# An encoder layer whose first projection takes its operands from a transposed copy of x

## What is computed

```python
u = rms_norm(h, g_pre_mix[l])     # h * rsqrt(mean(h*h) + EPS) * g
proj = jnp.einsum('bsd,de->bse', u, w_in[l])
sq, sk, sv, rx, rg, cq, ck, cv = jnp.split(proj, split_idx, axis=-1)
```

## Time and profile before

| | |
|---|---|
| median of 3 runs | 1148.42 us (1148.1 to 1149.21) |
| the profiled execution | 1147.69 us, its span 1146.0 us |
| TensorE busy | 1080.7 us (94%) |
| VectorE, ScalarE, GpSimd busy | 805.1, 574.7, 78.5 us |
| granted TensorE clock, mean | 0.974 of full speed |
| DMA | 70.44 MB, mean 61 GB/s |
| first projection matmul (L677) | 16.99 us after the span's start |

### The profile page before, as it was taken

How to read it: one execution, slowest core, us unless ns; L and a number is a source line. 1 busy time by engine, 2 the same in 40 slices (tenths; PEclk the granted TensorE clock), 3 DMA queues, 4 the chain that set the end, 5 groups by cost and what they waited for, 6 DMA issues and landing times.

```text
span 1146.0 us, 12155 instructions
## 1 busy us (share of the span) xinstructions
PE 1080.7 (94%) x4844; PEld 843.8 (74%) x4844; DVE 805.1 (70%) x778; ACT 574.7 (50%) x711; POOL 78.5 (7%) x70
## 2 busy tenths in 40 slices
PE   6999999997899999979999999999999999999993
PEld 5777777886445447857888888878888878888782
DVE  2535668656454544879778686799876898867998
ACT  6313432447455551575675446743466533467353
POOL 0004113201100101410000000000000000000000
PEclk9999999978899999988999999999999999999997
DMA  7221112110000025140220401301204013026003
GB/s 223 59 65 38 37 37 74 37 38 1 1 1 1 1 85 191 74 166 1 78 69 1 147 1 37 110 1 60 88 1 147 1 37 111 1 62 232 1 1 147
DMA packets 44640, 70.44 MB, mean 61 GB/s; under 512 B 10244, under 2 KB 19752, under 8 KB 44584
## 3 DMA queue, kind: packets, MB, share of 16 engines
q1 hardware_dynamic: 43544, 69.66, 18.0%
q10 hardware_dynamic: 1040, 0.00, 0.1%
HBM read 61.27 MB, written 8.39 MB: 61 GB/s over the span
## 4 chain that ended last, share of the span: by engine, by line
PE 81%; DVE 8%; ACT 6%; issue 2%; DMA 2%; SPq 1%; DVEq 0%; POOL 0%; ACTq 0%
PE ps L677 25%; PE ps L681 24%; PE ps L679 24%; PE ps L893 2%; PE ps L753 1%; PE ps L906 1%; ACT swa_p L1206 1%; PE ps L921 1%; PE ps L861 1%; DVE out_gained L1937 1%; DVE sb_e L1724 1%; ACT sb_e L1265 1%; DMA g_pre_mix_c<-in_g_pre_mix 1%; DVE ps L1758 1%; ACT sb_w L1245 1%
## 5 line engine op out<-in xcount | busy, mean ns | idle before, releaser
L677 PE MATMUL ps<-a_op,b_op 128*128 128x512 f32 x448 | 175.7, 392 | 5.7 <-DVE b_op L1854 4.8
L677 PE MATMUL ps<-b_op,a_op 128*128 128x512 f32 x448 | 174.6, 390 | 2.7 <-issue 2.7
L679 PE MATMUL ps<-a_op,b_op 128*128 128x512 f32 x448 | 175.3, 391 | 0.0
L681 PE MATMUL ps<-a_op,b_op 128*128 128x512 f32 x448 | 175.2, 391 | 0.0
L681 PE MATMUL ps<-b_op,a_op 128*128 128x512 f32 x448 | 174.3, 389 | 0.0
L679 PE MATMUL ps<-b_op,a_op 128*128 128x512 f32 x448 | 174.3, 389 | 0.0
L677 PE MATMUL ps<-act_hi,w_hi 128*128 128x512 f32 x288 | 115.0, 399 | 3.2 <-DVE w_lo L1516 3.2
L1382 ACT CAST a_op<-f 128x1024 fp32r<-128x1024 f32 x56 | 58.8, 1049 | 116.1 <-PE ps L681 75.9
L1854 DVE TENSOR_TENSOR b_op<-wq,b_op 128x1024 fp32r<-128x1024 f32 x96 | 117.0, 1218 | 0.0
L679 PE MATMUL ps<-act_lo,w_hi 128*128 128x512 f32 x288 | 112.8, 392 | 0.0
L681 PE MATMUL ps<-act_hi,w_lo 128*128 128x512 f32 x288 | 112.6, 391 | 0.0
(11 more groups left out here) (189 smaller groups left out, 1755.8 us busy)
## 6 DMA issues: line engine op xcount, KB each, us to landing
wq<-in_w_ff_in SPq DMA_DIRECT2D x16, 1024.0 KB, 5.4
wq<-in_w_ff_out SPq DMA_DIRECT2D x16, 1024.0 KB, 5.2
stage<-in_w_in SPq DMA_DIRECT2D x18, 512.0 KB, 4.7
y<-in_x SPq DMA_DIRECT2D x4, 1024.0 KB, 9.9
stage<-in_w_out SPq DMA_DIRECT2D x8, 512.0 KB, 3.8
h_spill<-y SPq DMA_DIRECT2D x8, 512.0 KB, 2.7
h_back<-h_spill SPq DMA_DIRECT2D x2, 2048.0 KB, 11.8
out<-y SPq DMA_DIRECT2D x8, 512.0 KB, 2.7
```

What stands on the lines that cost most here:

```text
L677: nc.tensor.matmul(dst, stat[0], mov[0], start=first, stop=False, skip_group_check=chained)
L679: nc.tensor.matmul(dst, stat[0], mov[1], start=False, stop=False, skip_group_check=chained)
L681: return nc.tensor.matmul(dst, stat[1], mov[0], start=False, stop=last, skip_group_check=chained)
```

## The change

The launch hands over two more arrays: `x_turned`, x transposed (4 MB), and `columns`, eight small vectors side by side as 128 x 56 numbers. They take the place of the eight vectors as inputs. In the kernel:

- x_turned is loaded into `xt`, which lies where `act_lo` lies, in five parts (`XT_PARTS`): half 0 in k slices 0-1, 2-3 and 4-7, half 1 in 0-3 and 4-7. ScalarE and VectorE read it there, and the rest is written over it. TensorE transposes nothing, and the functions `turn_inputs` and `first_granule` are gone. x itself is still loaded for the norms, later, in four parts of 256 tokens.
- The first two k slices' operands come after one half of the weights; the order of ScalarE and VectorE follows the parts.
- Granule 1 uses banks 4 to 7 (`proj_bank`), so its products don't wait for the copies of granule 0, and the norms are computed after all the splitting for granules 0 and 1; they are spread behind f = 4.
- The small product of the relative bias stands behind the first half's products, its copy before ScalarE's second half, and its way through DRAM before the gate loads. The band matmul stands behind f = 8.

```diff
+XT_PARTS = ((0, 0, 2), (0, 2, 4), (0, 4, 8), (1, 0, 4), (1, 4, 8))
...
+        xt = at("xt", [P, KD, S], ACT_AT + 32 * K)
...
+        def proj_bank(g, n, half):
+            return 2 * n + half + (4 if g == 1 else 0)
...
@@ SyncE
-            for half in range(2):
-                for c in range(2):
-                    cols = slice(BANK * c, BANK * (c + 1))
-                    sp.dma_start(y[:, 4 * half:4 * half + 4, cols],
-                                 x[0, BANK * half:BANK * (half + 1), cols]
-                                 .rearrange("(i p) d -> p i d", p=P)).then_inc(x_loaded[2 * half + c], 16)
-                load_in(half, w_in[0], IN_COLS[half])
...
+            sp.dma_start(columns_c[:, :], columns).then_inc(columns_loaded, 16)
+            load_in_half(0, 0)
+            load_turned(0)
+            load_turned(1)
+            load_in_half(0, 1)
+            load_turned(2)
+            sp.dma_start(onehot_c, onehot).then_inc(rel_loaded, 16)
+            sp.dma_start(rel_c[0:REL_BUCKETS, :], rel_bias).then_inc(rel_loaded, 16)
+            load_turned(3)
+            load_turned(4)
+            load_in(1, w_in[0], IN_COLS[1])
+            for i in range(4):
+                sp.dma_start(y[:, 2 * i:2 * i + 2, :], x[0, 2 * P * i:2 * P * (i + 1), :]
+                             .rearrange("(i p) d -> p i d", p=P)).then_inc(x_loaded[i], 16)
+            sp.wait_ge(rel_copied, 1)
+            sp.dma_start(rel_dram, rel_row).then_inc(rel_stored, 16)
+            sp.wait_ge(rel_stored, 16)
+            sliding = bass.AP(rel_dram.tensor, 0, [[1, CHUNK], [REL_SPAN + 1, 4], [1, P]])
+            sp.dma_start(rel_slide, sliding).then_inc(rel_back, 16)
...
@@ TensorE
-            first_granule(0, 0, proj_ready)
...
+            for half in range(HALVES):
+                for n in range(2):
+                    feature_major(0, n, half)
+                if half == 0:
+                    pe.wait_ge(rel_loaded, 32)
+                    nc.tensor.matmul(ps[0:4, 4, 0:REL_SPAN + 1], rel_c[0:REL_BUCKETS, :], onehot_c,
+                                     start=True, stop=True).then_inc(rel_summed, 1)
             for g in range(1, N_IN):
                 pe.wait_ge(w_lo_ready, 2 * (g + 1))
                 for half in range(HALVES):
                     for n in range(2):
-                        pe.wait_ge(proj_copied, 4 * g + 2 * half + n - 3)
-                        feature_major(g % 2, n, half, proj_ready)
+                        f = 4 * g + 2 * half + n
+                        if f == 4:
+                            pe.wait_ge(rel_copied, 1)
+                        elif f == 6:
+                            pe.wait_ge(rs_row_ready, 1)
+                        elif f >= 8:
+                            pe.wait_ge(proj_copied, f - 7 if g == 2 else f - 3)
+                        feature_major(g, n, half)
+                        if f == 4:
+                            spread_norms()
+                        if f == 8:
+                            pe.wait_ge(proj_copied, 8)
+                            pe.wait_ge(rel_back, 16)
+                            nc.tensor.matmul(ps[:, 5, :], flip, work[0:CHUNK, 2, 0:4 * P],
+                                             start=True, stop=True).then_inc(band_ready, 1)
...
@@ ScalarE
+            round_weights(0, 0)
+            act.wait_ge(columns_loaded, 16)
+            round_inputs(0)
+            round_inputs(1)
+            act.wait_ge(stage_loaded[1], 16)
+            round_weights(1, 0)
+            round_inputs(2)
+            act.wait_ge(rel_summed, 1)
+            nc.scalar.copy(rel_row, ps[0:4, 4, 0:REL_SPAN + 1]).then_inc(rel_copied, 1)
+            round_inputs(3)
+            round_inputs(4)
+            split_hi(1, 1)
...
@@ VectorE
+            rest_weights(0, 0, 0)
+            rest_inputs(0)
+            rest_inputs(1)
+            rest_weights(0, 1, 0)
+            rest_inputs(2)
+            rest_inputs(3)
+            rest_inputs(4)
+            split_lo(1, 1)
```

More of the change, by code:

```diff
@@ L161, in encoder_layer @@
         bias_band = const("bias_band", 4 * P)
[L162 to L172, removed]
+        columns_c = const("columns_c", sum(COLUMNS.values()))
+        first = [sum(list(COLUMNS.values())[:i]) for i in range(len(COLUMNS))]
+        g_pre_mix_c, g_pre_mlp_c, g_group_c, conv_w_c, conv_b_c, ba_c, bx_c, lam_c = (
+            columns_c[:, at:at + width] for at, width in zip(first, COLUMNS.values()))
+        lru_cols = const("lru_cols", 3 * LRU_TILES)
+        lam_t, decay_c, neg_decay_c = (
+            lru_cols[:, LRU_TILES * i:LRU_TILES * (i + 1)] for i in range(3))
         sink_c = const("sink_c", 4)
@@ L482, in _, with load_turned @@
[L482 to L494, removed]
+            def load_turned(i):
+                half, k0, k1 = XT_PARTS[i]
+                toks = slice(BANK * half, BANK * (half + 1))
+                sp.dma_start(xt[:, k0:k1, toks], x_turned[P * k0:P * k1, toks]
+                             .rearrange("(k p) n -> p k n", p=P)).then_inc(xt_loaded[i], 16)
@@ L682, in three_passes, with feature_major @@
                                         skip_group_check=chained)
[L684 to L699, removed]
+            def feature_major(g, n, half):
+                whi, wlo = w_slot(w_hi, g % 2, "in"), w_slot(w_lo, g % 2, "in")
                 for k in range(KD):
-                    if first is not None:
-                        pe.wait_ge(u_lo_ready, first + KD * half + k + 1)
+                    if g == 0:
+                        pe.wait_ge(u_lo_ready, KD * half + k + 1)
                         if k % 4 == 0:
-                            pe.wait_ge(w_lo_ready, 2 * g + k // 4 + 1)
+                            pe.wait_ge(w_lo_ready, k // 4 + 1)
                     cols = slice(P * n, P * (n + 1))
                     toks = slice(BANK * half, BANK * (half + 1))
-                    mm = three_passes(ps[:, 2 * n + half, :],
+                    mm = three_passes(ps[:, proj_bank(g, n, half), :],
                                       (whi[:, k, cols], wlo[:, k, cols]),
@@ L1065, in after, with round_weights @@
                 act.wait_ge(act_step, n_step[0])
+            def round_weights(s, slot):
+                nc.scalar.copy(w_hi[:, slot, 1024 * s:1024 * (s + 1)], stage[:, s, :])\
+                    .then_inc(w_hi_ready, 1)
             def split_hi(g, slot):
@@ L1097, in spread_copy @@
             def spread_copy():
-                act.wait_ge(rs_spread, spread_copy.n)
-                nc.scalar.copy(rs_row[:, :], ps[:, 6:8, :].rearrange("p b n -> p (b n)"))\
-                    .then_inc(rs_row_ready, 1)
-                spread_copy.n += 1
-            spread_copy.n = 1
+                act.wait_ge(rs_spread, 1)
+                for half in range(2):
+                    ins = nc.scalar.copy(rs_row[:, BANK * half:BANK * (half + 1)],
+                                         ps[:, 5 + 2 * half, :])
+                ins.then_inc(rs_row_ready, 1)
             def group_rsqrt(grp):
@@ L1142, in _ @@
             nc.scalar.activation(lam_t[:, :], lam_t[:, :], ACT.Ln, bias=1.0).then_inc(lam_ln, 1)
-            round_inputs(0, 1, g_pre_mix_c)
+            act.wait_ge(eps_ready, 1)
+            for i in range(TOK):
+                if i % 2 == 0:
+                    act.wait_ge(x_loaded[i // 2], 16)
+                squares(i, work[:, 4, :])
+            first_rsqrt(slice(0, TOK), 0)
             spread_copy()
-            split_hi(1, 1)
             def recurrent(c):
@@ L2041, in _, with laid_out @@
                 final_tile(i)
-INPUTS = ["x", "g_pre_mix", "w_in", "conv_w", "conv_b", "lru_wa", "lru_ba", "lru_wx", "lru_bx",
-          "lru_lambda", "swa_sinks", "rel_bias", "g_group", "w_out", "g_post_mix", "g_pre_mlp",
-          "w_ff_in", "w_ff_out", "g_post_mlp"]
+INPUTS = ["x", "w_in", "lru_wa", "lru_wx", "swa_sinks", "rel_bias", "w_out", "g_post_mix", "w_ff_in",
+          "w_ff_out", "g_post_mlp"]
+def laid_out(inputs):
+    by_partition = [np.asarray(inputs[name])[0].reshape(-1, P).T for name in COLUMNS]
+    return {"onehot": bucket_onehot(),
+            "x_turned": np.ascontiguousarray(np.asarray(inputs["x"])[0].T),
+            "columns": np.ascontiguousarray(np.concatenate(by_partition, axis=1))}
 def kernel(**inputs):
@@ L2054 @@
     arrays, args = {}, []
[L2055 to L2056 removed]
+    more = laid_out(inputs)
+    for name in [*INPUTS, *more]:
+        a = more[name] if name in more else np.ascontiguousarray(inputs[name])
         arrays[f"in_{name}"] = a
```

126 lines of the change are left out of this document (45 added, 81 removed).

## The result

| | before | after |
|---|---|---|
| median of 4 runs each, on one chip | 1148.82 us (1148.1 to 1149.37) | 1138.89 us (1137.68 to 1141.42) |
| ratio of after to before | | 0.9917, 95% interval 0.9897 to 0.9936 |
| the profiled execution | 1147.69 us, span 1146.0 | 1141.42 us, span 1139.7 |
| TensorE busy | 1080.7 us | 1072.8 us |
| DMA | 70.44 MB | 74.62 MB |

The change takes 9.9 us off; the forecast was 8.7 (1139.7 us). The transposing of x has not become cheaper: the launch does it, outside the measured time, and the kernel pays 4.18 MB more of transfers for it.

What follows compares the result with a forecast made beforehand. TensorE was taken as the bound, with 11.5 us of early waits. Followed to f = 8 and the band, 76.4 became 67.7, gain 8.7: 1147.69 - 8.7 = 1139.0, plus 0.73 for the median, 1139.7 us; range 1137.6 to 1142.6.

Steps and rivals of the forecast that it cites:

- Landing: DMA queues at the start: 0.37 MB/us, first weights landed at 5.3 us, x_turned parts at 6.8, 8.2 and 12.5.
- rival B: Operands at the start land late, at 0.27 MB/us, 3.2 us later: gain 5.5, 1142.9 us; chance 0.09.
- First half: First half of the tokens: first matmul at 8.45 instead of 16.99, a 1.25 us gap before slice 4, bias product ended 22.6.
- Second half: Second half of the tokens: TensorE pauses 1.8 us before slice 8, behind the bias row's copy, then no further gap.
- the third pause: TensorE waiting for the norms (rstd) after f = 4, near 41 us: 2.3 us.
- SBUF or PSUM: Slices read from SBUF, not PSUM: 0.69 us kept, 0.1 either way per slice, -1.0 to +1.0 us on the gain.
- The norms: Norms inside the second granule: rstd at 43.0, wanted at 40.8, spread by 44.8; f = 8 and band done at 67.7.
- What cost nothing: Copies and longer SP queue before f = 8: third granule's weights split by 54, wanted at 61.2, cover 7 us.
- rival C: Third granule's weights come too late on the SP queue, f = 8 starts 14.9 us later: 1154.6 us; chance 0.03.
- Rival A: TensorE's clock falls after a gap, 1.6 us paid at the first or third: gain 7.1, 1141.3 us; chance 0.26.
- the second gap: TensorE's 1.8 us pause before slice 8; a fall of the clock there is absorbed because the third gap shrinks.
- Rival D: Later stages meet the clock better or norms come sooner: 1 to 2 us either way, 1138 us; chance 0.10.

Runs made afterwards that it cites:

- again: The changed kernel, unedited, measured once more: 1139.73 us, ratio 0.993 to the kernel before.
- turned_only: The changed kernel with the eight small vectors loaded one by one again instead of in one array: 1139.1 us, ratio 0.9922 to the kernel before.
- weights_late_7: The changed kernel with SyncE waiting for the seventh product (f = 6) before issuing the third granule's weights: 1144.02 us, one run.
- big_parts: The changed kernel with the first two 0.5 MB parts of x_turned joined into one of 1 MB: 1141.07 us, ratio 0.9941 to the kernel before.
- copy_late: The changed kernel with ScalarE's copy of the bias row moved behind its sixteenth slice: 1135.17 us, ratio 0.9886 to the kernel before.
- warm: The changed kernel with 28 small identity matmuls ahead of the first product: 1139.2 us, ratio 0.9925 to the kernel before.
- weights_late_6: The changed kernel with SyncE waiting for the sixth product (f = 5) before issuing the third granule's weights: 1138.61 us, one run.
- weights_late_8: The changed kernel with SyncE waiting for the eighth product (f = 7) before issuing the third granule's weights: 1152.82 us, one run.
- old_banks: The changed kernel with granule 1 back in banks 0 to 3 and the norms spread ahead of f = 4: 1149.91 us, ratio 1.0022 to the kernel before.
- vectors_only: The kernel before with only its eight small vectors put in one array, x still turned on TensorE: 1141.53 us, ratio 0.9945.

## Why the prediction was right, step by step

*Landing.* The vectors took 0.39 us of the queue (0.5 said). Weights: ScalarE took the first half at 5.33 (5.3). Slice 0 at 7.25 (6.8), slice 4 at 12.90 (12.5). The rate between 4 and 30 us, by stretches:

```profile
4.00:12.00 8.00, 3.14 (x8) 2.49 (x9) 4.82 (x6) 4.75 (x6) 0.00 (x0) 1.00 1.06 374
12.00:20.00 8.00, 7.86 (x30) 5.82 (x29) 3.11 (x5) 2.57 (x4) 0.00 (x0) 1.00 1.07 372
20.00:30.00 10.00, 8.19 (x37) 6.09 (x36) 5.59 (x9) 6.56 (x11) 0.00 (x0) 1.00 1.03 407
```

The 0.37 MB/us that the sum took is what was moved, in parts of 0.5 MB too. This is what refutes **rival B** (0.27 MB/us, 3.2 us late); the Trainium skill ("DMA: Bandwidth & Descriptors", Bandwidth) asks for 1 MB or more a transfer, and with several of half that size queued one behind the other the trace doesn't show the loss.

*First half.* First matmul 8.86, 8.26 in again (8.45). The eight slow matmuls were twelve in after, turned_only and weights_late_7, and seven or eight in again, big_parts and copy_late; that is paid out of the pause before slice 4, forecast at 1.25 us (0.1 us left in after, 0.9 in again), as warm shows. Slice 4 at 14.46 for 14.0, the bias product at 22.99 for 22.2; again has 13.81 and 22.29. The term was 0.1 to 0.8 short: slices 4 to 7 were taken 0.4 us later than forecast in after (0.25 earlier in again), and from slice 4 to the bias product it took 8.5 us for 8.2.

*Second half.* The pause came as said, at its place, for the copy (1.81 us for 1.8), and VectorE supplied a slice in 0.67 us. copy_late shows its cause by itself. What the prediction didn't say is that the same copy is also the cause of the third pause: take it away and both go.

*SBUF or PSUM.* The same 128x512 operation has a median of 687 ns on ScalarE and 740 on VectorE from PSUM, 710 and 748 from SBUF. Over ten slices that is 0.2 to 0.3 us, inside the bound of 1.0.
*The norms.* rstd at 43.5 (43.0), pause 1.69 (2.3), because TensorE came later too. Spread ended at 45.63 (44.8). Third granule: f = 8 with the band at 68.46 and 67.76 (67.7). **Gain at that point 7.94 and 8.64, for 8.7.** So the mechanism and its size came out. That the median (1138.89) also lies within 0.8 us of the forecast of 1139.7 is in part luck, since what the later stages add or take is of that size and was not forecast in the sum.

*What cost nothing.* Gate loads over at 43.2 (46), the weights behind them ready at 51.6 (54): a cover of 10.3 us, where 7 was said. weights_late_6, _7 and _8 show that it is real and what lies beyond it: **rival C** was told rightly as a mechanism, but its price leaves out the fall of the clock, which came with both pauses (eight to ten matmuls at 0.43 us, 1.6 to 2 us more).

**Rival A, the clock after a gap.** It came, and in the way that the forecast left room for: at the second gap, where it is absorbed. Stretches of 25 to 29 us in again and in after:

```profile
25.00:29.00 4.00, 4.00 (x13) 3.05 (x12) 4.00 (x7) 4.00 (x7) 0.00 (x0) 0.57 1.03 410
```

```profile
25.00:29.00 4.00, 3.79 (x16) 3.07 (x17) 4.00 (x7) 4.00 (x7) 0.00 (x0) 1.00 1.03 410
```

Behind the same pause of 1.8 us the clock fell in five of nine profiles (again, turned_only, old_banks, weights_late_6 and _8) and not in after, big_parts, warm and weights_late_7. Where it fell the pause on the norms is 0 to 0.2 us and not 1.7, and the spread begins at 42.84 to 43.46; where it didn't, at 43.08 to 43.60 (old_banks, with its own long pause, apart). So length alone doesn't decide; vectors_only, with no fall after 3.25 us, says the same. The Trainium skill ("TensorE: Matmul & The Clock Gate", Part 1) says that the same kernel changes speed at different points, and the profiles of after and again agree. Here the fall costs nothing.

**Rival D, the later stages.** They are why the profile shows 6.3 us of span and not 7.94. Why the median, with 9.9 us, lies on the other side no profile shows. In after the clock fell inside the 64 matmuls of the landmark, 5 us earlier in the work than before (there it fell at the pause of the earlier trace rows):

```profile
228.00:230.00 2.00, 1.37 (x7) 0.79 (x5) 0.59 (x1) 0.59 (x1) 0.00 (x0) 1.00 0.00 0
230.00:232.00 2.00, 1.85 (x36) 1.85 (x38) 1.61 (x3) 1.42 (x2) 0.00 (x0) 1.00 0.00 0
232.00:234.00 2.00, 2.00 (x33) 2.00 (x28) 1.97 (x5) 0.00 (x0) 0.00 (x0) 0.68 0.55 159
234.00:236.00 2.00, 2.00 (x12) 1.67 (x10) 1.93 (x5) 0.00 (x0) 0.00 (x0) 0.50 0.84 254
...
240.00:245.00 5.00, 4.61 (x23) 4.62 (x23) 1.39 (x3) 4.42 (x15) 0.50 (x2) 0.50 0.00 0
```

The 64 take 4.67 us for 3.71, and by the pause of the earlier trace rows (240.39 for 245.66) only 5.27 of the 7.94 us are left. Over 14 profiles, from the landmark to the end of the span takes between 905.3 us (copy_late) and 911.2 (weights_late_8), with 907.9 before and 909.5 after. By the transposes ahead of the MLP twelve of them divide alike: landmark to there takes 276.9 to 280.3 us, from there to the end 628.2 to 629.4, so most of the spread is in the attention and recurrence stages. In weights_late_6 and _8, of one run each, it is 275.9 and 279.8 us to there, and 631.4 behind it. Which edit moves it which way stays open; no run here shows a rule, and one kernel's four runs spread by 3.7 us. What the change itself gives is the 7.9 to 8.6 us ahead of the landmark; by the medians it gives 9.9, and 7.9 in again (against 1147.59), and what these differ by from the landmark's gain is not shown to be its doing.

## What to carry to other kernels

When a change moves the start of a chain, follow it on the trace's clock to the first point that both kernels pass with the same work done, and compare there: the medians mix it with stages whose time spreads by several us from run to run. Ask of each part of a change what it gives alone; parts that cut the same wait overlap (6 and 8 gave 8 to 10). And look in each engine's list for a small step that waits in front of work that could go: one 0.31 us copy held eight slices and the norms, and moving it was worth about 4 us.

## What the runs showed that was not expected

- After pauses of 2.4, 5.8 and 7.9 us the clock fell, after 1.8 us in five of nine profiles, and after pauses of 3.2 us ahead of the first projection matmul it fell in the kernel before and not in vectors_only. And in after it fell between 232 and 234 us, with TensorE busy for 1.85 of the two microseconds before, behind a wait of 0.79 us alone.
- At the very start the granted clock of the page doesn't show what the matmuls do: after's twelve first ones stand 0.43 us apart, the pace of 1.2 GHz, in a stretch whose column reads 1.00. The distance between matmuls is the surer sign there.
- The first matmul can come 1.0 us later (big_parts) or 2.4 (warm) and the band within 0.3 us of after, because the landing of slices 4 to 7 sets it. Between after and again that landing itself is 0.65 us apart, and the band 0.7.
- Small vectors loaded one by one cost the kernel before 6 us, though their queue time looked idle: 8.73 us for the 4 KB gain (4.5 in turned_only), and a VectorE that stood for 11.8 us behind the last of them.
